# Starting the product behind a norm before the norm is known, in a two-block network on one core

## The reference

```python
def rms_norm(x, g):
    y = xf * lax.rsqrt(jnp.mean(xf * xf, axis=-1, keepdims=True) + EPS)
    return (y * g.astype(jnp.float32)).astype(x.dtype)

def modulate(t, sub):
    return rms_norm(t, norm_g[layer, sub]) * (1.0 + mod[:, sub, 1]) + mod[:, sub, 0]

h = modulate(x, 0)
x = x + HALF_STEP * (1.0 + mod[:, 0, 2]) * swiglu(h, ffn_w_gate[layer, 0], ffn_w_up[layer, 0], ffn_w_down[layer, 0])
```

## Time and profile before

| | us |
|---|---|
| median of 3 runs | 3599.61 |
| lowest and highest | 3599.25, 3606.14 |
| the profiled execution's time | 3600.31 |
| its span | 3598.5 |
| PE busy | 3466.9 |
| DVE busy | 1980.1 |
| ACT busy | 1183.8 |
| POOL busy | 364.9 |
| mean granted TensorE clock | 0.973 of full speed |

### The profile page before, as it was taken

How to read it: one execution, slowest core, us unless ns; L and a number is a source line. 1 busy time by engine, 2 the same in 40 slices (tenths; PEclk the granted TensorE clock), 3 DMA queues, 4 the chain that set the end, 5 groups by cost and what they waited for, 6 DMA issues and landing times. The chain is left out here.

```text
span 3598.5 us, 56173 instructions
## 1 busy us (share of the span) xinstructions
PE 3466.9 (96%) x22376; PEld 2799.2 (78%) x22376; DVE 1980.1 (55%) x2770; ACT 1183.8 (33%) x1733; POOL 364.9 (10%) x264
## 2 busy tenths in 40 slices
PE   7999999999999999999999999999989999999998
PEld 4888777878888788876678788887768787878886
DVE  6665566756654666465343433355667773454343
ACT  3222245433222322233242322233434542233231
POOL 1000003410000000010101000130103330010000
PEclk9999999999999999999899999999989999989999
DMA  6555322125554555421032223222210002223332
GB/s 248 196 189 178 113 77 73 56 89 189 198 193 138 181 187 202 160 84 50 1 104 95 86 96 109 89 83 84 63 39 6 8 6 71 95 64 98 89 100 70
DMA packets 103764, 382.74 MB, mean 106 GB/s; under 512 B 11424, under 2 KB 15136, under 8 KB 103200
## 3 DMA queue, kind: packets, MB, share of 16 engines
q1 hardware_dynamic: 103584, 380.15, 31.4%
HBM read 378.01 MB, written 2.10 MB: 106 GB/s over the span
## 5 line engine op out<-in xcount | busy, mean ns | idle before, releaser
L401 PE MATMUL bank<-h_hi,w_hi 128*128 128x512 f32 x2616 | 1031.4, 394 | 20.3 <-DVE w_lo L246 17.5
L402 PE MATMUL bank<-h_lo,w_hi 128*128 128x512 f32 x2616 | 1021.8, 391 | 0.0
L403 PE MATMUL bank<-h_hi,w_lo 128*128 128x512 f32 x2616 | 1021.8, 391 | 0.0
L246 DVE TENSOR_TENSOR w_lo<-w_raw,w_hi 128x1024 fp32r<-128x1024 f32 (+2 forms) x480 | 645.9, 1346 | 512.4 <-ACT w_hi L240 502.6
L240 ACT ACTIVATE w_hi<-w_raw 128x1024 fp32r<-128x1024 f32 (+2 forms) x480 | 526.5, 1097 | 345.3 <-PE bank L403 283.5
L401 PEld LDWEIGHTS bank<-h_hi,w_hi 128*128 128x128 f32 x2616 | 493.2, 189 | 138.0 <-DVE w_lo L246 23.3
L403 PEld LDWEIGHTS bank<-h_hi,w_lo 128*128 128x128 f32 x2616 | 493.0, 188 | 104.3
L402 PEld LDWEIGHTS bank<-h_lo,w_hi 128*128 128x128 f32 x2616 | 493.5, 189 | 102.3 <-issue 1.9
L401 PE MATMUL bank<-f_gu_hi,w_hi 128*128 128x512 f32 x704 | 279.4, 397 | 0.0
L403 PE MATMUL bank<-f_gu_hi,w_lo 128*128 128x512 f32 x704 | 279.1, 396 | 0.0
L402 PE MATMUL bank<-f_gu_lo,w_hi 128*128 128x512 f32 x704 | 279.1, 396 | 0.0
(11 more groups left out here) (618 smaller groups left out, 4604.8 us busy)
## 6 DMA issues: line engine op xcount, KB each, us to landing
ada_tiles<-in_ada SPq DMA_DIRECT2D x180, 512.0 KB, 4.1
w_raw<-in_gu SPq DMA_DIRECT2D x176, 512.0 KB, 4.4
w_raw<-in_dn SPq DMA_DIRECT2D x64, 704.0 KB, 4.2
w_raw<-in_w_ff SPq DMA_DIRECT2D x64, 512.0 KB, 3.6
w_raw<-in_w_hyb SPq DMA_DIRECT2D x36, 512.0 KB, 3.4
w_raw<-in_w_rkv SPq DMA_DIRECT2D x24, 512.0 KB, 3.5
w_raw<-in_w_attn SPq DMA_DIRECT2D x20, 512.0 KB, 3.6
w_raw<-in_w_hout SPq DMA_DIRECT2D x16, 512.0 KB, 3.4
```

What stands on the lines that cost most here:

```text
L246: K.nc.vector.tensor_tensor(K.w_lo[:, half, 0:kb * P], K.w_raw[:, slot, 0:kb * P], K.w_hi[:, half, 0:kb * P].bitcast(F32), ALU.subtract).t ...
L401: nc.tensor.matmul(K.ps[bank][:], wh, hi, start=start, stop=False)
L402: nc.tensor.matmul(K.ps[bank][:], wh, lo, start=False, stop=False)
L403: last_mm = nc.tensor.matmul(K.ps[bank][:], wl, hi, start=False, stop=stop)
```

## The change

**Ahead of the norm.** In the `project` before each of the five norms, DVE and ACT make h_hi and h_lo of each finished chunk of the residual from gain times residual, without the row of roots and without the shift (`ahead_act`, `ahead_dve`). The squares move to another place, since h_hi now holds these.

**Tile 0 early.** TensorE first multiplies tile 0's raw weights by the shift, one column (`shift_products`). Then it multiplies tile 0 by the early h, with the sums of squares behind chunk 1 and the row of roots behind chunk 3 (in the last norm behind chunk 7). ACT copies the bank out, DVE multiplies the copy by the row back into the bank, and ACT adds the shift's share as a bias.

**Tiles 1 and 2.** They take the place of the interleaved pair (`next_pair`): all h_hi matmuls of tile 1, those of tile 2, then the h_lo matmuls of both. The third tile's weights are split inside the norm, between chunks (`third_weights`). SP waits for the shift product before it loads over tile 0's raw weights.

The core of the diff:

```diff
+            def early_tile():
+                pe.wait_ge(K.lo_done.sem, g0 + PRIMED + 1)
+                pe_wait(pe, 0, 0, 0)
+                head.shift_products(pe)
+                for k in range(kb):
+                    pe.wait_ge(K.h_ready.sem, K.h_ready(k + 1 - kb))
+                    hi, lo, bank, start, stop = mm(k, 0)
+                    wh, wl = weights(0, k)
+                    nc.tensor.matmul(K.ps[bank][:], wh, hi, start=start, stop=False)
+                    nc.tensor.matmul(K.ps[bank][:], wh, lo, start=False, stop=False)
+                    last_mm = nc.tensor.matmul(K.ps[bank][:], wl, hi, start=False, stop=stop)
+                    last_mm.then_inc(K.early_read.sem, 1)
+                    head.between(pe, k)
+                head.behind(pe)
+
+            def next_pair():
+                for j in (1, 2):
+                    pe.wait_ge(K.lo_done.sem, g0 + j + PRIMED + 1)
+                    pe_wait(pe, 0, j, j)
+                    for k in range(kb):
+                        pe.wait_ge(K.h_hi_done.sem, K.h_hi_done(k + 1))
+                        hi, lo, bank, start, stop = mm(k, j)
+                        wh, wl = weights(j, k)
+                        nc.tensor.matmul(K.ps[bank][:], wh, hi, start=start, stop=False)
+                        nc.tensor.matmul(K.ps[bank][:], wl, hi, start=False, stop=False)
+                pe.wait_ge(K.tile_mm.sem, done0 + 1)
+                for j in (1, 2):
+                    for k in range(kb):
+                        hi, lo, bank, start, stop = mm(k, j)
+                        pe.wait_ge(K.h_ready.sem, K.h_ready(k + 1))
+                        last_mm = nc.tensor.matmul(K.ps[bank][:], weights(j, k)[0], lo, start=False, stop=stop)
+                    last_mm.then_inc(K.tile_mm.sem, 1)
...
+            if early:
+                sp.wait_ge(K.early_mm.sem, K.early_mm(1))
...
+            def third_weights():
+                act.wait_ge(K.w_loaded[2], 16 * ((g0 + 2) // RING + 1))
+                act.wait_ge(K.early_read.sem, K.early_read(kb))
+                nc.scalar.activation(K.w_hi[:, 0, 0:kb * P], K.w_raw[:, 2, 0:kb * P], ACT.Copy).then_inc(K.hi_done.sem, 1)
...
     def clear(self, pool):
+        if self.vacated:
+            pool.wait_ge(*self.vacated)
...
+    def ahead_act(self, act, o):
+        K = self.K
+        K.nc.scalar.activation(K.h_hi[:, bass.ds(o, 1), :], K.x[:, bass.ds(o, 1), :], ACT.Identity, scale=K.gain[:, bass.ds(o, 1)]).then_inc(K.h_hi_done.sem, 1)
+
+    def ahead_dve(self, dve, o):
+        K = self.K
+        dve.wait_ge(K.h_hi_done.sem, K.h_hi_done(o + 1))
+        K.nc.vector.scalar_tensor_tensor(K.h_lo[:, bass.ds(o, 1), :], K.x[:, bass.ds(o, 1), :], K.gain[:, bass.ds(o, 1)],
+                                         K.h_hi[:, bass.ds(o, 1), :].bitcast(F32), ALU.mult, ALU.subtract).then_inc(K.h_ready.sem, 1)
...
+    def shift_products(self, pe):
+        K = self.K
+        pe.wait_ge(K.bank_free.sem, K.bank_free(-1))
+        for c in range(DC):
+            last = K.nc.tensor.matmul(K.ps[self.SUM][:, 8:9], K.w_raw[:, 0, c * P:(c + 1) * P], self.shift[:, c:c + 1],
+                                      start=c == 0, stop=c == DC - 1, skip_group_check=True)
+        last.then_inc(K.early_mm.sem, 1)
+
+    def between(self, pe, k):
+        if k == 1:
+            self.parts = self.K.sq_parts
+            self.sums_pe(pe)
+        if k == self.ROW_AFTER:
+            self.row_of_roots(pe)
...
+    def early_act(self, act, second_weights, third_weights):
+        K = self.K
+        second_weights()
+        self.rms_act(act)
+        for c in range(DC):
+            act.wait_ge(K.scaled.sem, K.scaled(c + 1))
+            K.nc.scalar.activation(K.h_hi[:, c, :], K.t[:, c, :], ACT.Identity, bias=self.shift[:, c:c + 1]).then_inc(K.h_hi_done.sem, 1)
+            if c == 3:
+                third_weights()
+                K.nc.scalar.activation(K.t[:, DC - 1, :], K.ps[0][:], ACT.Copy).then_inc(K.early_copied.sem, 1)
+            if c == 4:
+                act.wait_ge(K.early_fixed.sem, K.early_fixed(2))
+                K.nc.scalar.activation(K.ps[0][:], K.ps[0][:], ACT.Identity, bias=K.early_bias[:, 0:1]).then_inc(K.tile_mm.sem, 1)
+
+    def early_dve(self, dve, second_weights, third_weights):
+        K, v = self.K, self.K.nc.vector
+        second_weights()
+        self.rms_dve(dve)
+        dve.wait_ge(K.early_mm.sem, K.early_mm(1))
+        v.tensor_copy(K.early_bias[:], K.ps[self.SUM][:, 8:9]).then_inc(K.early_fixed.sem, 1)
+        dve.wait_ge(K.rms_row.sem, K.rms_row(1))
+        for c in range(DC):
+            if c == DC - 1:
+                dve.wait_ge(K.early_fixed.sem, K.early_fixed(2))
+            dve.wait_ge(K.early_read.sem, K.early_read(c + 1))
+            v.scalar_tensor_tensor(K.t[:, c, :], K.x[:, c, :], K.gain[:, c:c + 1], K.ps[self.ROW][:], ALU.mult, ALU.mult).then_inc(K.scaled.sem, 1)
+            if c == 4:
+                dve.wait_ge(K.early_copied.sem, K.early_copied(1))
+                v.tensor_tensor(K.ps[0][:], K.t[:, DC - 1, :], K.ps[self.ROW][:], ALU.mult).then_inc(K.early_fixed.sem, 1)
+                third_weights()
+        for c in range(DC):
+            dve.wait_ge(K.h_hi_done.sem, K.h_hi_done(c + 1))
+            v.scalar_tensor_tensor(K.h_lo[:, c, :], K.t[:, c, :], self.shift[:, c:c + 1], K.h_hi[:, c, :].bitcast(F32),
+                                   ALU.add, ALU.subtract).then_inc(K.h_ready.sem, 1)
...
             act.wait_ge(free.sem, free(o + 1))
+            if follow:
+                act.wait_ge(K.x_written.sem, K.x_written(follow.GAIN_STEPS))
             squares.by_act(act, K.x[:, bass.ds(o, 1), :], o, j // tpo % 2)
+            if follow:
+                follow.ahead_act(act, o)
...
+            if step == "f11":
+                follow = final_head(K)
+            elif step != "hyb":
+                follow = Modulated(K, *terms(K, *places[plan[n + 1]]), early=True)
```

More of the change, by code:

```diff
@@ L278, in gemm @@
     done0 = g0 + PRIMED
+    early = head and head.early
     with one_block(K) as block:
@@ L362, in _ @@
         def _(pe):
-            if head:
+            if head and not early:
                 head.pe(pe)
@@ L530, with __init__ @@
 class Squares:
-    def __init__(self, K, name, base, per=2, gain=None):
-        self.K, self.per = K, per
+    def __init__(self, K, name, base, per=2, gain=None, vacated=None):
+        self.K, self.per, self.vacated = K, per, vacated
         self.gain = K.cols_at[gain][0] if gain else None
@@ L611, in sums_pe @@
                 a = n * NT + t
-                mm(total[:, a:a + 1], acc[:, t * P:(t + 1) * P], K.ones[:, 0:1], start=a == 0, stop=False, skip_group_check=True)
+                mm(total[:, a:a + 1], acc[:, t * P:(t + 1) * P], K.ones[:, 0:1], start=a == 0 and not self.early, stop=False, skip_group_check=True)
         pe.wait_ge(K.sq_done.sem, K.sq_done(0))
@@ L636, with __init__, gain_ahead @@
 class Modulated(Rms):
-    def __init__(self, K, gain, scale, shift):
+    ROW_AFTER = 3
+    def __init__(self, K, gain, scale, shift, early=False):
         super().__init__(K)
-        self.gain, self.scale, self.shift = gain, scale, shift
+        self.gain, self.scale, self.shift, self.early = gain, scale, shift, early
+    def gain_ahead(self, dve):
+        K = self.K
+        dve.wait_ge(K.x_written.sem, K.x_written(0))
+        K.nc.vector.scalar_tensor_tensor(K.gain[:], self.scale, 1.0, self.gain, ALU.add, ALU.mult).then_inc(K.x_written.sem, 1)
+        dve.wait_ge(K.x_written.sem, K.x_written(1))
@@ new lines, in between, with behind @@
+    def between(self, pe, k):
[4 more added lines that the diff above has]
+            self.row_of_roots(pe)
+    def behind(self, pe):
+        pass
+    def early_act(self, act, second_weights, third_weights):
+        K = self.K
+        second_weights()
[9 more added lines that the diff above has]
+                K.nc.scalar.activation(K.ps[0][:], K.ps[0][:], ACT.Identity, bias=K.early_bias[:, 0:1]).then_inc(K.tile_mm.sem, 1)
@@ L672, in advance @@
         self.rms_advance()
-        self.K.x_written.base += 1
+        if self.early:
+            for c, n in ((self.K.early_mm, 1), (self.K.early_read, DC), (self.K.early_copied, 1), (self.K.early_fixed, 2)):
+                c.base += n
+        else:
+            self.K.x_written.base += 1
         for c in (self.K.scaled, self.K.h_hi_done, self.K.h_ready):
@@ L878, in __init__ @@
     def __init__(self, K, gain, scale, shift, final, row):
-        super().__init__(K, gain, scale, shift)
+        super().__init__(K, gain, scale, shift, early=True)
         self.final, self.row = final, row
@@ L882, in __init__, with gain_ahead, behind @@
         self.r, self.both = K.final_small
-    def pe(self, pe):
+    GAIN_STEPS = 2
+    ROW_AFTER = None
+    def gain_ahead(self, dve):
+        super().gain_ahead(dve)
+        K = self.K
+        K.nc.vector.tensor_tensor(K.gain[:], K.gain[:], self.final, ALU.mult).then_inc(K.x_written.sem, 1)
```

(30 more changed lines are left out.)

89 lines of the change are left out of this document (58 added, 31 removed).

## The result

The change made the kernel slower by a little: median **3610.48 us** (3604.84 to 3619.88, 12 runs) against 3600.15 (3594.39 to 3609.01, 12 runs) for the kernel before beside it. The ratio is **1.0027**, 95% interval 1.0016 to 1.0037. That set of the kernel before was a short one: four later sets of 17 to 29 runs had medians of 3604.57 to 3607.22. So the change costs something, but how much is less firm than the interval says. The profiled execution took 3611.86, with a span of 3610.1; before it was 3600.31 and 3598.5.

A forecast was written before the change was run, and what follows sets the result against it. TensorE, busy 96% of the span, was taken to set the end. Three like norms +0.9, f11 +1.2 and the last norm +4.9 sum to +7.0 us on the 3599.6 median: 3606.6 us, range 3597 to 3615.

The forecast's parts named there:

- Part 1: In a norm, from the last large matmul to DVE's scaling behind the row of roots: 7.9 us, against 5.8 before.
- Part 2: From start of scaling to the fourth weight tile: 18.4 us, TensorE starving some 3.5; norm 26.3 against 27.2 at high clock.
- Part 3: One low stretch of TensorE's clock per norm, behind the starvation, costing 1.2 us, bounds 0 and 2.4.
- Rival A: Slower: the clock falls ahead of the row too, in shift product and sums; 2 us in four norms, 3614.6; chance 0.15.
- Part 4: Last norm: more sum passes, row behind all of tile 0, two low stretches; 33.1 us against 28.2, so +4.9.
- Part 5: Product before each norm: the added ACT and DVE operations stay hidden and cost nothing, 0.7 us to spare at the tightest.
- rival B: Slower: product before stalls, DVE held for POOL's whole operation in ml and f11; 17 us, so 3623; chance 0.07.
- C: Faster: TensorE doesn't starve in the norms as ScalarE and DVE overlap more; 3 us in four norms, 3590; chance 0.10.
- D: No change: the clock never falls in the norms; -0.4 us in all, 3599.2; chance 0.18.

The follow-up runs named there:

- fill_starve: Changed kernel with 3 and 8 idle 128x512 matmuls, results unread, put where TensorE starves in the norms; 3612.34 us, ratio 1.0025 to the kernel before.
- ahead_only: Kernel before plus the change's ahead work in the five products before a norm, norms as before, ahead halves overwritten unread; 3595.54 us, ratio 0.9975.
- shift_late: Changed kernel with the shift products moved from ahead of the new product to behind the row of roots; 3591.26 us, ratio 0.9974 to the kernel before.
- before_again: The kernel before, unedited, profiled once more for the spread of its own profile; 3606.48 us.

## Why the prediction was right, and where it was not

The median came out 10.9 us above the one I started from, and 3.9 above my 3606.6: inside the range, on the slower side of my 0.2%. Against the runs beside it, it is 10.3. By the parts:

**Part 1 (7.9 us to the scaling): right, where the clock holds.** 7.8 in ml. The row's passes took 1.05 instead of 0.9.

**Part 2 (18.4 from the scaling to the fourth tile, starvation 3.5): right.** In ml 19.8 with the low stretch, 18.2 less its 1.6; starvation 1.04 + 1.93 = 3.0, at the chunks named. fill_starve's 26.0 for ml is my 26.3 without a fall. What the sum lacked was the tile after: the work that DVE put off inside the norm delays the fifth tile's low half, 1.4 us in hyb and ml, 3.6 over the five norms. My interval ended one tile too early to see it.

**Part 3 (1.2 for the clock behind the starvation): right in kind, 1.6 in size.** The Trainium skill (TensorE: Matmul & The Clock Gate, Why this matters for your kernels) warns of idle gaps between bursts, and the trace agrees: low stretches of 3.4 to 6.8 us behind the starvation in all five norms. In hyb and f10 the stretch was 6.8 us long and the way from the scaling to the fourth tile 20.5 and 20.6 instead of 18.2, so it cost 2.3 to 2.4 there, my upper bound.

**Rival A was no rival but a part of the truth.** I set it at 0.15 for four norms and priced it at 2 us. It came in two norms of the profile, and cost 5.3 in each: the scaling starts 4.5 later, since everything to the row runs at half speed, and the second low stretch was 6.8 us instead of 3.4 long. The step that failed is the argument against it, that twelve large matmuls stand between the short products. With the shift products, 2 us of one-column work, directly behind the last product, the clock fell ahead of the row in 9 of 24 norms; with them behind the row, in 0 of 8. Those twelve large matmuls stand there in both. ml's norm has the same order as the hybrid's and kept the clock, so the place doesn't decide alone.

**Part 4 (last norm +4.9): +4.4 between the two profiles, but by luck.** 32.6 against the 33.1 forecast; the 28.2 of before was low, as six more profiles with that norm in its old order and without idle matmuls show (30.7 to 31.9). Against those it is +0.6 to +1.9 in this trace and up to +5 in the second. I had counted two low stretches; the first profile has one, behind the starvation, and only the second has both (35.8). What the sum lacked is POOL: in this norm its work on the residual draws DVE's eight low halves out from 5.38 to 8.31. With the clock held behind the scaling (fill_starve) this norm still took 20.6 from there to the fourth tile, the four others 18.2, and TensorE waited for `h_lo`. In the changed kernel's first profile it took 20.6 as well, with the low stretch lying over that wait. So the 2.6 for the clock stood in for 2.4 that POOL costs in any case. The 28.2 was the one profile in which DVE went first: a term taken from one trace held the chance of that trace.

**Part 5 (ahead work costs nothing): right**, by ahead_only, and **rival B's stall did not happen**. But I set it aside by a wrong reading. The earlier trace rows don't show less than an exclusion: the low half of ml started at 1930.02 in a POOL operation that ended at 1930.49, so only 0.47 of the 1.3 was left, and it lost 0.32. A row of before with more of the operation left, beside one of POOL:

```profile
3159.83 1.29 POOL L560 TENSOR_TENSOR sq_acc_mix<-sq_acc_mix,sq_mix 128x512 f32<-128x512 f32 x1 [6.29 <-DVE sq_mix L553]
3160.01 2.19 DVE L246 TENSOR_TENSOR w_lo<-w_raw,w_hi 128x1024 fp32r<-128x1024 f32 x1 [0.26 <-ACT w_hi L240]
```

Here 1.11 was left and DVE lost 0.96. Of the 35 such low halves in that trace that start inside a single POOL operation, 33 lost what was left of it (0.39 to 1.24 us) less 0.14 to 0.15. The Trainium skill (SBUF — State Buffer, Who interferes with whom) has the two exclude each other for a whole instruction, and the trace agrees: one of them waits. The ahead work was cheap because of when it comes. In ml, DVE's h_lo starts with 0.68 of POOL's operation left and takes 1.23 instead of 0.75; the weights' low half behind it then finds POOL idle and takes 1.21 instead of 1.55. In f11, with two POOL operations, h_lo takes 1.87, so it is held for 1.1, and the low half 1.61 instead of 2.27. That leaves both products without a gap.

**Rivals C and D** were the cases of a kernel that the experiments then made: with the clock held (shift_late) the four norms take 24.0 to 24.5, as C had it (half of the way to 21.5), but not for C's reason: the shift products left the path, and the clock stayed high. D's sum without any fall, 26.3 a norm, fits the unchanged order (26.0 in fill_starve) and was 2 us too high for shift_late's, as the row comes earlier there.

**The total was right partly by compensation.** The norms cost 21.3 in the trace and not 7.0. The heads of ml gave back 9.6 and the small gaps 3.2. Of the remaining stages one (the second block's mixer) cost 5.7 more than in the first profile, but before_again has 5.9 there too; most of the rest is 2 us less ahead of the first of the five norms and 2 us less behind that mixer. The total can't be called evidence for my sum; the intervals of ml, f11 and of the experiments can.

## What to carry to other kernels

Work that fills a gap on TensorE must not stand ahead of what ends the gap: eight one-column products in front of the row cost more than the early tile brought, and behind it they cost nothing. Before rebuilding a stage to fill it with real work, price the clock apart from the emptiness with idle matmuls: here a few lines of them gave the same 0.4% as the rebuilt norms. Then look where a gain lies before you credit an edit with it: in both kernels about half of it or more came in a stage that no edit touched. And take such terms from several profiles: one norm's interval differed by 3 us between two of the same kernel, for the order of two engines.

## What was unexpected of the hardware

A fall of the clock can lock into a loop: mLSTM heads of 34.1 us each met one every time, and those of 30.7 none, through most of the stage; whether an edit elsewhere or chance decides which is not shown. Idle matmuls of 128x512 kept the granted clock at 2.4 GHz in 9 of 11 norms of the kernel before in which they were put, where one-column products let it fall. DVE's two-input operations and POOL's ran one after the other, and with the same starts one profile gave POOL the wait (5.07) and another DVE (8.30 instead of 5.38), which was worth 2.8 us of a norm. And products that no edit touches ran 0.9 ns per matmul faster in every kernel with the new code, 3 to 4 us in all, for a cause left open.
